# 32 of 256 tokens leave two streamed expert matrices: gathered rows on VectorE, and matrix 2 with its weights stationary

## What is computed

```
s = einsum('thpc,pkc->thpk', q, sub_keys)            # 8 heads, 2 halves, 128 keys
s1, i1 = top_k(s[:, :, 0], 16); s2, i2 = top_k(s[:, :, 1], 16)
sc, ci = top_k(s1 + s2 (all 256 pairs), 16)
e = i1[ci // 16] * 128 + i2[ci % 16]                 # 8 x 16 experts of each token
g = softmax(sc)
act = gelu(einsum('td,thkd->thk', xb, expert_u[e]))
out = einsum('thk,thkd->td', g * act, expert_v[e])
x = x + out;  return rms_norm(x, final_norm_g)
```

## Time and profile before

| | us |
|---|---|
| median of 3 runs | 1251.67 (1251.4 to 1252.78) |
| the profiled execution | 1253.08 |
| its span, first to last instruction | 1251.2 |

### The profile page before, as it was taken

One profiled execution on the slowest core, in us unless ns is written; L12 is line 12 of the kernel. 1 busy time (PEld: TensorE's weight loads), 2 busy tenths in 40 slices (PEclk: granted clock), 3 DMA queues, 4 the chain that ended last, 5 costly groups with the idle time before them and its releaser, 6 DMA issues.

```text
span 1251.2 us, 21981 instructions
## 1 busy us (share of the span) xinstructions
PE 1238.5 (99%) x8585; PEld 1127.5 (90%) x8585; DVE 940.7 (75%) x1706; ACT 689.3 (55%) x1153; POOL 34.3 (3%) x29
## 2 busy tenths in 40 slices
PE   8999999999999999999999999999999999999998
PEld 7799989998888889999999999999988888888886
DVE  5886668774458767999999888888776767676676
ACT  6676467663466754454555556556545454545454
POOL 0000220000020010000000000000000000000000
PEclk9999999999999999999999999999999999999999
DMA  8644556666557436477777665665667666666662
GB/s 280 205 145 135 153 177 205 199 193 194 194 150 247 135 116 209 156 250 249 242 237 245 219 225 186 220 202 190 244 256 274 229 245 234 236 247 252 243 251 95
DMA packets 73127, 261.61 MB, mean 209 GB/s; under 512 B 8320, under 2 KB 8832, under 8 KB 72768
## 3 DMA queue, kind: packets, MB, share of 16 engines
q1 hardware_dynamic: 71552, 256.30, 60.5%
q0 software_dynamic: 1040, 3.34, 0.8%
q10 hardware_dynamic: 432, 0.56, 0.1%
HBM read 241.29 MB, written 18.87 MB: 208 GB/s over the span
## 4 chain that ended last, share of the span: by engine, by line
PE 90%; DVE 4%; DMA 2%; ACT 2%; issue 1%; SPq 0%; DVEq 0%; ACTq 0%
PE ps L1189 27%; PE ps L557 15%; PE ps L558 14%; PE ps L559 14%; PE ps L549 13%; PE ps L1152 2%; DVE wlo L1742 1%; PE ps L594 1%; DMA raw<-in_w_in_a_dram 1%; ACT whi L1232 1%; PE ps L607 1%; DVE turned_x L2081 1%; PE ps L1111 1%; DMA raw<-in_w_in_dram 1%; PE ps L624 1%
## 5 line engine op out<-in xcount | busy, mean ns | idle before, releaser
L1232 ACT ACTIVATE whi<-raw 128x1024 fp32r<-128x1024 f32 (+2 forms) x420 | 441.7, 1053 | 453.5 <-PE ps L559 199.9
L1742 DVE TENSOR_TENSOR wlo<-raw,whi 128x1024 fp32r<-128x1024 f32 (+2 forms) x409 | 495.6, 1215 | 232.8 <-ACT whi L1232 230.0
L557 PE MATMUL ps<-turned_x,whi 128*128 128x256 f32 x1504 | 419.0, 279 | 0.0
L558 PE MATMUL ps<-turned_x,whi 128*128 128x256 f32 x1504 | 416.0, 277 | 0.0
L559 PE MATMUL ps<-turned_x,wlo 128*128 128x256 f32 x1504 | 415.9, 277 | 0.0
L1189 PE MATMUL ps<-whi,turned_x 128*128 128x512 f32 x1024 | 315.6, 389 | 0.0
L557 PEld LDWEIGHTS ps<-turned_x,whi 128*128 128x128 f32 x1504 | 282.6, 188 | 0.7 <-issue 0.5
L558 PEld LDWEIGHTS ps<-turned_x,whi 128*128 128x128 f32 x1504 | 282.8, 188 | 0.0
L559 PEld LDWEIGHTS ps<-turned_x,wlo 128*128 128x128 f32 x1504 | 282.4, 188 | 0.0
L1189 PEld LDWEIGHTS ps<-whi,turned_x 128*128 128x128 f32 x1024 | 192.2, 188 | 39.9
L1189 PE MATMUL ps<-wlo,turned_x 128*128 128x512 f32 x512 | 199.2, 389 | 0.0
(11 more groups left out here) (354 smaller groups left out, 1197.8 us busy)
## 6 DMA issues: line engine op xcount, KB each, us to landing
raw<-in_expert_u_dram SPq DMA_DIRECT2D x128, 512.0 KB, 4.4
raw<-in_expert_v_dram SPq DMA_DIRECT2D x128, 512.0 KB, 5.0
raw<-in_w_up_dram SPq DMA_DIRECT2D x32, 512.0 KB, 4.2
raw<-in_w_down_dram SPq DMA_DIRECT2D x32, 512.0 KB, 3.7
acts<-stage SPq DMA_DIRECT2D x32, 512.0 KB, 3.0
stage<-acts SPq DMA_DIRECT2D x30, 512.0 KB, 3.3
raw<-in_w_in_dram SPq DMA_DIRECT2D x20, 512.0 KB, 4.1
raw<-in_w_gate_dram SPq DMA_DIRECT2D x16, 512.0 KB, 3.5
```

Of the source, the lines that this page charges most:

```text
L557: e.matmul(dst, whi[:, h, sl], xh[:, k, :], start=k == 0, stop=False)
L558: e.matmul(dst, whi[:, h, sl], xl[:, k, :], start=False, stop=False)
L1232: e.activation(whi[:, u % NH, 0:n], raw[:, u % NR, 0:n], ACT.Copy).then_inc(*hi(u))
L1742: e.tensor_tensor(wlo[:, u % NH, 0:n], raw[:, u % NR, 0:n], whi[:, u % NH, 0:n].bitcast(F32), ALU.subtract).then_inc(*lo(u))
```

## The change

- The last 32 tokens (224 to 255) leave both expert matrices. The other 224 (DENSE) stay: products of matrix 1 have 224 columns, the gates are 56 groups (GROUPS), gelus and `cut` are 128x224.
- The 32 tokens' 4096 rows of each matrix come by 64 indirect DMAs from GpSimd's queue, 128 rows of 4 KB each (4 experts for each of the 32 tokens), into a ring of three buffers. VectorE forms one dot product for each partition (rows of expert_u) or adds a scaled row to `held` (rows of expert_v), one 128x1024 operation a fetch. `rows_from` and `rows_due` place them: the first 32 one in two units of matrix 1, from unit 62 on, the other 32 one in 3.25 units of matrix 2, from unit 6 on.
- Matrix 2 is turned around: 8 chunks of 128 columns of the weights are held; the high weights take both parts of the activations in one product (2 x 224 columns), the low weights the high part alone. It uses all 8 PSUM banks, and the result stands with columns on partitions, so at the end ScalarE and VectorE add the two parts and TensorE transposes 8 blocks back (`turn_end`).
- GpSimd makes the low part of 16 units, every third from EU+4 to EU+49. VectorE's routing has 1.75 us a unit in place of 1.35, and TURN_AT and HOT_FROM come at 53 and 55 in place of 67 and 69.
- The end: both token halves are finished together; GpSimd makes a part of the final gain.

```diff
-UB1 = 1.35
+DENSE = 224
+GROUPS = DENSE // 4
+UB1 = 1.75
...
-LO_POOL = (BR_B + 1, BR_B + 2, BR_B + 3, OUT, OUT + 1, UP, UP + 1, IN2, IN2 + 1, QUERY, QUERY + 1)
-EXP_AT, TURN_AT, HOT_FROM = 45, 67, 69
+LO_POOL = (BR_B + 1, BR_B + 2, BR_B + 3, OUT, OUT + 1, UP, UP + 1, IN2, IN2 + 1, QUERY, QUERY + 1,
+           *range(EU + 4, EU + 50, 3))
+EXP_AT, TURN_AT, HOT_FROM = 36, 53, 55
...
+def rows_from(r):
+    return EU + 58 + 2 * r if r < 32 else EV + 2 + 13 * (r - 32) // 4
+def rows_due(u):
+    return [r for r in range(64) if rows_from(r) + 4 == u]
...
+        THL = turned_x[:, 0:4096].rearrange("p (w k n) -> p w k n", w=2, n=256)
...
-        low4 = ACTV[:, 80:88, :].rearrange("p a b -> p (a b)")
+        room4 = sb(p4, "ACTV", [128, 128, 256])
+        ACTV = room4[:, 0:112, :].rearrange("p a b -> p (a b)").rearrange("p (u t) -> p u t", t=DENSE)
+        spare4 = room4[:, 112:128, :].rearrange("p a b -> p (a b)")
+        row_ring, held = [spare4[:, a:a + 1024] for a in (0, 1024, 3072)], spare4[:, 2048:3072]
+        packed = spare4[96:128, 1280:1408].bitcast(I32)
+        sums4 = room4[:, 0:8, :]
+        low4 = room4[:, 80:88, :].rearrange("p a b -> p (a b)")
...
-                m = cols(EU + n, 0, 8, TH, TL, ps[b][:, 0:256], range(4))
+                m = cols(EU + n, 0, 8, TH[:, :, 0:DENSE], TL[:, :, 0:DENSE], ps[b][:, 0:DENSE], range(4))
                 if n == 127:
                     m.then_inc(*half_used("u"))
-                cols(EU + n, 0, 8, TH, TL, ps[b][:, 0:256], range(4, 8)).then_inc(*used(EU + n))
+                cols(EU + n, 0, 8, TH[:, :, 0:DENSE], TL[:, :, 0:DENSE], ps[b][:, 0:DENSE], range(4, 8)).then_inc(*used(EU + n))
...
-            def accumulate(n, t, d):
-                h, sl = (EV + n) % NH, slice(t * 128, t * 128 + 128)
-                for k, (x, w) in enumerate(((RH, whi), (RH, wlo), (RL, whi))):
-                    m = e.matmul(ps[bank4(t, d)][:, :], x[:, n % 8, sl], w[:, h, d * 512:d * 512 + 512],
-                                 start=n == 0 and k == 0, stop=n == 127 and k == 2)
-                return m
+            def accumulate(n, c):
+                h, sl = (EV + n) % NH, slice(c * 128, c * 128 + 128)
+                e.matmul(ps[c][:, 0:2 * DENSE].rearrange("p (w t) -> p w t", w=2), whi[:, h, sl], THL[:, :, n % 8, 0:DENSE],
+                         start=n == 0, stop=False)
+                return e.matmul(ps[c][:, 0:DENSE], wlo[:, h, sl], TH[:, n % 8, 0:DENSE], start=False, stop=n == 127)
+            def turn_end(c):
+                e.wait_ge(*end_d.at(f"c{c}"))
+                for t in range(2):
+                    m = e.transpose(ps[c][:, t * 128:t * 128 + 128], sums4[:, c, t * 128:t * 128 + 128], ident)
+                m.then_inc(*turned(f"end{c}"))
             for n in range(125):
                 whole(EV + n)
                 e.wait_ge(*cut_d.at(n))
                 if n == 0:
-                    e.wait_ge(*weight_a.at(63))
-                for t in range(2):
-                    for d in range(2):
-                        m = accumulate(n, t, d)
+                    e.wait_ge(*weight_a.at(GROUPS - 1))
+                for c in range(8):
+                    if n == 0 and c > 3:
+                        e.wait_ge(*gelu_u.at(120 + c))
+                    m = accumulate(n, c)
                 m.then_inc(*used(EV + n))
-            for n in range(125, 127):
+            for n in range(125, 128):
                 whole(EV + n)
                 e.wait_ge(*cut_d.at(n))
-                for d in range(2):
-                    accumulate(n, 0, d)
-            whole(EV + 127)
-            e.wait_ge(*cut_d.at(127))
-            for t in range(2):
-                for d in range(2):
-                    for n in range(125 if t else 127, 128):
-                        m = accumulate(n, t, d)
-                    m.then_inc(*ended(2 * t + d))
+                for c in range(4):
+                    m = accumulate(n, c)
+                    if n == 127:
+                        m.then_inc(*ended(c))
+            for c in range(4, 8):
+                for n in range(125, 128):
+                    m = accumulate(n, c)
+                m.then_inc(*ended(c))
+                if c == 4:
+                    for i in range(4):
+                        turn_end(i)
+                else:
+                    turn_end(c - 1)
+            turn_end(7)
...
+                if n == 1:
+                    e.wait_ge(*row_d.at("dot31"))
+                    e.activation(row_act, row_dot, ACT.Gelu_apprx_tanh).then_inc(*row_a("gelu"))
...
+            for c in range(7):
+                take_low(c)
+            e.wait_ge(*lo.at(UNITS - 1))
+            end_squares(0, 0, 6)
+            take_low(7)
+            end_squares(1, 6, 7)
+            end_squares(2, 7, 8)
+            e.wait_ge(*end_d.at("v"))
...
+            def row_products(u):
+                for r in rows_due(u):
+                    k, rows_in = r % 32, row_ring[r % 3]
+                    if r == 0:
+                        e.wait_ge(*row_p.at("gain"))
+                    if r == 32:
+                        e.wait_ge(*row_a.at("gelu"))
+                        e.wait_ge(*d_gate.at(0))
+                        e.tensor_tensor(row_act, row_act, row_gate, ALU.mult).then_inc(*row_d("act"))
+                        e.wait_ge(*row_d.at("act"))
+                    e.wait_ge(*d_rows[r % 3].at(r))
+                    if r < 32:
+                        e.tensor_tensor_reduce(rows_in, rows_in, held, 1.0, 0.0, ALU.mult, ALU.add,
+                                               row_dot[:, k:k + 1]).then_inc(*row_d(f"dot{k}"))
+                    elif k == 0:
+                        scaled_copy(held, rows_in, row_act[:, 0:1]).then_inc(*row_d("sum0"))
+                    else:
+                        e.wait_ge(*row_d.at(f"sum{k - 1}"))
+                        e.scalar_tensor_tensor(out=held, in0=rows_in, scalar=row_act[:, k:k + 1], in1=held, op0=ALU.mult,
+                                               op1=ALU.add).then_inc(*row_d(f"sum{k}"))
...
+                row_products(EV + n)
+                if n == 60:
+                    e.memset(sums4[:, :, DENSE:256], 0.0).then_inc(*end_d("zero"))
+                if n >= 119 and n < 123:
+                    if n == 119:
+                        e.wait_ge(*d_back.at(0))
+                        e.wait_ge(*d_four.at(0))
+                    else:
+                        e.wait_ge(*end_d.at(f"rows{n - 120}"))
+                    e.tensor_tensor(X[96:128, 1, :], X[96:128, 1, :], spare4[96:128, 1024 * (n - 119):1024 * (n - 118)], ALU.add).then_inc(
+                        *end_d(f"rows{n - 119}"))
...
+            for u in range(EU + 4, EU + 50, 3):
+                split(u)
...
+            for c in range(4):
+                e.dma_start(held[32 * c:32 * c + 32, :], x_kept[96:128, 1, :]).then_inc(*d_held(c))
+                e.dma_start(row_r[32 * c:32 * c + 32, :], r_kept).then_inc(*d_scale(c))
...
+            def fetch_rows(r):
+                e.wait_ge(*hi.at(rows_from(r)))
+                if r > 2:
+                    e.wait_ge(*row_d.at(f"dot{r - 3}" if r < 35 else f"sum{r - 35}"))
+                table, k = (A["expert_u_rows"], r) if r < 32 else (A["expert_v"], r - 32)
+                e.indirect_dma_start(out=row_ring[r % 3], out_offset=None, in_=table,
+                                     in_offset=bass.IndirectOffsetOnAxis(ap=row_at[:, k:k + 1], axis=0)).then_inc(*d_rows[r % 3](r))
...
+            e.tensor_scalar(held, held, row_r, None, ALU.mult).then_inc(*row_p("x"))
+            e.wait_ge(*row_p.at("x"))
+            e.tensor_tensor(held, held, row_ring[2], ALU.mult).then_inc(*row_p("gain"))
+            e.wait_ge(*row_p.at("gain"))
+            for r in range(64):
+                fetch_rows(r)
+                if r == 36:
+                    e.wait_ge(*cut_d.at(4))
+                    e.dma_start(gb4, A["final_norm_g_2"].partition_broadcast(128)).then_inc(*d_gb4(0))
+            e.wait_ge(*row_d.at("sum31"))
+            e.dma_start(shares.rearrange("c t n -> (c t) n"), held).then_inc(*d_shares(0))
+            e.wait_ge(*d_shares.at(0))
+            e.dma_start(spare4[96:128, :].rearrange("t (c n) -> t c n", c=4), shares.rearrange("c t n -> t c n")).then_inc(*d_four(0))
+            e.wait_ge(*d_gb4.at(0))
+            e.wait_ge(*lo.at(UNITS - 1))
+            for i, c0, c1 in ((0, 0, 512), (1, 512, 768)):
+                for t in range(2):
```

190 lines of the change are left out of this document (122 added, 68 removed), and 1 row of the table turned.

## The result

| | median us (runs) | profiled execution | its span |
|---|---|---|---|
| before | 1252.22 (1251.4 to 1252.82, 4) | 1253.08 | 1251.2 |
| changed | 1264.59 (1262.82 to 1268.17, 4) | 1264.99 | 1263.2 |

The ratio is 1.0103, 95% interval 1.0079 to 1.0126: the change is 1% slower, where 1222 us (1186 to 1242) were forecast, 30 us faster.

What follows compares the result with a forecast made beforehand. TensorE's rate was taken as the bound, with VectorE next. Matrix 2 -29.0, matrix 1 -5.0, one-hot groups -3.8, unhidden work +3 and the end +5 gave -29.8: 1222 us, range 1186 to 1242.

Steps and rivals of the forecast that it cites:

- The rate: Matrix 1: 24 products at 111.7 ns make a unit 2.68 us in place of 2.72, about -5 us.
- Late matrix 1: Units 52 to 128 of matrix 1: shorter units and eight fewer one-hot groups, -7 us.
- The traffic of matrix 2: Matrix 2: 785 KB a unit in 2.49 us, 315 GB/s, a DMA share of 0.85.
- The end: After the last product: transposes +1.9 and serial finishing work +3, together +5 us (3 to 8).
- The fourth rival: Matrix 2 products charged as 512 and 256 columns, so no gain there: 1251 us or a little more; chance 0.04.
- matrix 2's rate: Matrix 2: eight product pairs make a unit 2.49 us in place of 2.72, -29.0 us over 128 units.
- The split within a pair: Matrix 2: the 448-column product takes 200 ns, the 224-column one 111.7.
- Load slack: Matrix 2: the load behind `fetch` loses 0.7 us of slack; 1 to 2 us late are covered, cost 0.
- GpSimd's splits: Matrix 1: 16 splits of 2.39 us fit three TensorE units; possible waits of VectorE counted in the +3.
- the +3: Work not hidden, +3 us: scratch adds at units 119 to 122 and GpSimd's splits; late loads also counted here.
- The second rival: Matrix 1: GpSimd's splits block VectorE 2.39 us each, up to +33 us; put at 1237 to 1256; chance 0.13.
- The third rival: Serial gathers pace VectorE, TensorE waits; at 8 us each +61, 1283 us; chance 0.06.

Runs made afterwards that it cites:

- x4: Changed kernel without the 32 tokens' row work and GpSimd's 16 splits, routing back at 1.35 us a unit: 1225.92 us, 0.978 of before.
- y2: Changed kernel with each fetch behind two loads in matrix 2, routing at 1.45 us a unit, row products moved later: 1226.07 us, 0.979 of before.
- x1: Changed kernel with each fetch of activations issued behind the next two loads of matrix 2 instead of ahead: 1241.73 us, 0.991 of before.
- x10: Kernel of x1 with GpSimd subtracting only 16 columns of each of its 16 units: 1225.96 us, 0.979 of before.

## Why the prediction was wrong

**Right.** *The rate*: 2.680 us a unit in matrix 1. *Late matrix 1*: -7.5 where VectorE leaves it alone (x4, y2), by units and groups -6.8. The traffic of matrix 2: 316 GB/s in x1 for 315, though at a DMA share of 0.92 and not 0.85. *The end*: +5.6 for +5, in part by luck. The timeline of the changed kernel's end answers to the earlier trace rows; 6.6 us lie between the last product's start and the issue of the last outputs, 3.2 before. So that path, to which the forecast gave all of its +5 ("8 us or so"), grew by 3.4, and 2.2 lie ahead of the last product and behind the issue:

```profile
1252.17 0.27 PE L1227 MATMUL ps<-turned_x,wlo 128*128 128x224 f32 x1
...
1258.79 0.95 ACTq L1791 DMA_DIRECT2D out_dram<-raw  x2
```

*The fourth rival* is out.

The timeline of matrix 2 in y2_mid_pool:

```profile
999.75 0.38 PE L1225 MATMUL ps<-turned_x,whi 128*128 128x448 f32 x1
999.97 0.27 PE L1227 MATMUL ps<-turned_x,wlo 128*128 128x224 f32 x1
1000.07 0.37 PE L1225 MATMUL ps<-turned_x,whi 128*128 128x448 f32 x1
...
1001.33 0.37 PE L1225 MATMUL ps<-turned_x,whi 128*128 128x448 f32 x1
```

**A term mis-sized: matrix 2's rate.** Five pairs in 1.58 us are 316 ns a pair, 311.7 forecast; a unit is 2.53 us where 2.49 stood. Over 124 units it is -22.4 instead of -28. (Of less weight: eight groups at 0.467 are 3.7, not 3.8.) The split within a pair was wrong as well: 0.22 and 0.10, not 0.20 and 0.11.

**The step that failed first: *Load slack*, "Cost 0".** Its numbers were right: the slack vanished (29 of 29 loads behind a fetch were waited for, against 3 before), and ScalarE waited for expert_v as foretold. What was wrong is that a late load was taken as a single event against buffers of three units. The fetch it queues behind waits for `take`, which waits, through VectorE's order, for that very load's split. Lateness in a ring isn't absorbed, it is the period: the question was whether landing, ScalarE's split, VectorE's two splits, two `take`s, a `cut`, a scaled add and the issue fit into four units. That sum was never made. With the earlier trace rows's 5.0 us for a landing and the 4.8 and 6.0 measured above it gives 9.8 of 10.0 without an add and 11.0 with one; even with 4.2, the median landing of the loads behind a fetch in the kernel before, a round with an add is 10.2. The gathers then made the landings longer, 4.3 to between 5.2 and 5.6. Price: 21.8 us.

**The step that failed second: *GpSimd's splits*, in the +3.** The second rival had the mechanism, its place (a late VectorE during the routing, TensorE waiting for `wlo`) and a price of up to 30; it measured 14.6 (x1 157.8, x10 143.2), and got a chance of 0.13. The reason it lost, "the order keeps splits apart", looked at splits beside splits in step. But VectorE was at 96% by plan, the routing's operations with two inputs lie beside GpSimd's splits as well, and each collision makes VectorE later, which would bring the next of its own splits beside GpSimd's (that last step is argued, not measured). The Trainium skill's page SBUF — State Buffer, section SBUF: two separate sides, calls the shared pair of ports an exclusive lock for a whole instruction; 2.80 in place of 1.22 us agrees. Operations that read one input were not lengthened: 12 of the 83 FIND_INDEX8 of this stretch lay wholly inside a split of GpSimd and took 285 to 421 ns, the others 281 to 422.

**The third rival** (gathers pace VectorE) didn't happen: VectorE has no wait for the ring of rows. In x1 a gather landed after 5.3 us (rows of expert_u) or 8.1 us (expert_v) by the median, which a ring of three buffers and the early issue covered. The gathers did harm by another way, through the landings of ordinary loads, which I had judged by the DMA engines' share alone.

With both losses out, the forecast's own sum comes out: y2's span is 26.8 us under before's, in parts -2.2, -7.5, -22.4, +5.4; 29.8 were forecast. That they are so close has luck in it: the +3 for work that isn't hidden wasn't needed and made up for half of what matrix 2's rate fell short. The prices of the work were right to within 6 us of 33, and the sign was wrong for two waits. One of the two was already in the program and only became a bound; the forecast saw it and priced it at 0, and no rival had it.

## What to carry to other kernels

Where a transfer queues behind one that waits for an engine, follow that wait round: if it comes back to the transfer, add up the whole round, with the landing at the load that the change will bring, and compare it with the time of the work it serves. No buffer covers a ring that is longer than that, and moving the waiting transfer behind the free one may be all that is needed (two lines here, 22 us). Work given to GpSimd relieved VectorE here only where VectorE had time to spare: in early matrix 1, 16 splits were free at 85% load, and at a planned 96% they gave back 17.4 of the 19.5 us that they took.

## What the runs showed of the hardware

- GpSimd waits for VectorE as well. Of x10_short_pool, GpSimd's subtractions of 16 columns, minimum, median and maximum in ns:

```profile
L2680 POOL TENSOR_TENSOR wlo<-raw,whi x16: 217/641/1274, 521.1 to 643.5; 128x16 fp32r<-128x16 f32 x16
```

The same small work took 217 or up to 1274 ns, about a split of VectorE's more.

- An indirect DMA of 512 KB keeps GpSimd for 1301 ns (matrix 1's rows) or 1740 (matrix 2's) by the mean of 32 each, and doesn't lengthen VectorE's operations: its splits in late matrix 1 and matrix 2 of the changed kernel stay at 1.22 us by the mean, the longest at 1.30.
- DMA engines at a share of 0.93, 326 GB/s, still fed TensorE without a gap (y2). In x1, at 0.92 and 316 GB/s and without a gap too, the loads of 512 KB of matrix 2 took 3.8 us to land at the least, 5.7 by the median and 9.2 at the most.
- Idle TensorE costs once more in its clock. The changed kernel, 3 us with a gap and the stretch behind it:

```profile
594.00:597.00 3.00, 0.43 (x4) 0.24 (x3) 2.97 (x2) 1.30 (x2) 0.00 (x0) 0.93 0.11 44
597.00:603.40 6.40, 6.24 (x29) 6.24 (x30) 6.19 (x21) 0.68 (x1) 0.00 (x0) 0.50 0.64 190
```

After 2.73 us of idleness the granted clock was 0.50, 1.2 GHz: 29 products in 6.40 us, where 6.40 / 0.1117 = 57 would have stood: the gap cost some 3 us more behind it.
- Why a product of 448 columns and one of 224 take 316 ns together, neither 298 (672 columns at the 0.443 ns of the earlier trace rows) nor 312, wasn't tried and stays open.
